# First four MLP units on half the tokens during the last normalisation, then on the other half

## The reference

```python
o = o @ w_out[l]
x = x + gt_a * rms_norm(o, g_post_attn[l])

h = rms_norm(x, g_pre_mlp[l]) * (1.0 + sc_m) + sh_m
y = jnp.square(jax.nn.relu(h @ w_mlp_in[l])) @ w_mlp_out[l]
x = x + gt_m * rms_norm(y, g_post_mlp[l])
```

## Time and profile before

| | before |
|---|---|
| median of 3 runs | 2115.51 us (2113.52 to 2116.0) |
| the profiled execution: its own time | 2116.55 us |
| its span, first to last instruction | 2114.9 us |
| PE busy | 2061.8 us, 97% |
| DVE busy | 1497.9 us, 71% |
| ACT busy | 844.0 us, 40% |
| mean granted TensorE clock | 0.991 |

### The profile page before, as it was taken

The page is one execution under the profiler, slowest core; times in us unless marked ns, Lnnn a source line. Parts: engine busy times, 40 slices in busy tenths (PEclk is TensorE's granted clock), DMA queues, the critical chain, the costliest instruction groups (busy, mean ns, idle before and its releaser), DMA issues.

```text
span 2114.9 us, 26212 instructions
## 1 busy us (share of the span) xinstructions
PE 2061.8 (97%) x9314; PEld 1703.6 (81%) x9314; DVE 1497.9 (71%) x1804; ACT 844.0 (40%) x1153; POOL 151.3 (7%) x159
## 2 busy tenths in 40 slices
PE   6999999999999989999999999999999999999998
PEld 6787888887788878888888888888788888888886
DVE  5986898788877776445544554435789888888866
ACT  4454322587732363333222332233333333333422
POOL 0000000038600000000000000012000000000000
PEclk8999999999999999999999999999999999999999
DMA  8997868600277737655665566676657356456442
GB/s 296 341 307 221 274 202 251 197 22 11 91 258 251 245 123 249 206 189 200 223 222 186 182 218 228 201 237 224 246 225 265 135 214 258 151 206 238 179 179 80
DMA packets 214353, 435.20 MB, mean 206 GB/s; under 512 B 30180, under 2 KB 69768, under 8 KB 205448
## 3 DMA queue, kind: packets, MB, share of 16 engines
q1 hardware_dynamic: 196136, 361.43, 50.8%
q0 software_dynamic: 16704, 67.11, 8.9%
q10 hardware_dynamic: 1440, 5.70, 0.7%
HBM read 367.09 MB, written 67.11 MB: 205 GB/s over the span
## 4 chain that ended last, share of the span: by engine, by line
PE 83%; DVE 7%; DMA 3%; issue 3%; ACT 3%; POOL 1%; SPq 0%; DVEq 0%; ACTq 0%; POOLq 0%
PE bank L2085 11%; PE bank L2087 11%; PE bank L2086 11%; PE bank L2522 7%; PE bank L2523 7%; PE bank L2524 7%; PE bank L2072 6%; PE bank L2074 6%; PE bank L2073 6%; DMA raw<-in_w_ada 1%; PE bank L2573 1%; PE bank L2571 1%; PE bank L2572 1%; DMA w<-in_w_mlp_out 1%; PE bank L2143 1%
## 5 line engine op out<-in xcount | busy, mean ns | idle before, releaser
L1241 DVE TENSOR_TENSOR lo<-raw,hi 128x1024 fp32r<-128x1024 f32 (+2 forms) x234 | 275.6, 1182 | 377.2 <-ACT hi L728 375.2
L728 ACT ACTIVATE hi<-raw 128x1024 fp32r<-128x1024 f32 (+2 forms) x236 | 239.4, 1023 | 657.5 <-PE bank L2087 410.7
L2085 PE MATMUL bank<-h_hi,hi 128*128 128x512 f32 x1016 | 396.0, 390 | 0.0
L2087 PE MATMUL bank<-h_hi,lo 128*128 128x512 f32 x1016 | 395.3, 389 | 0.0
L2086 PE MATMUL bank<-h_lo,hi 128*128 128x512 f32 x1016 | 395.2, 389 | 0.0
L2522 PE MATMUL bank<-hi,y_use 128*128 128x512 f32 x784 | 307.6, 392 | 7.7 <-DVE acc L1968 3.8
L2523 PE MATMUL bank<-lo,y_use 128*128 128x512 f32 x784 | 306.2, 391 | 0.0
L2524 PE MATMUL bank<-hi,y_use 128*128 128x512 f32 x784 | 306.1, 390 | 0.0
L1184 ACT ACTIVATE hi<-w 128x1024 fp32r<-128x1024 f32 x168 | 178.3, 1062 | 296.8 <-PE bank L2524 218.3
L1892 DVE TENSOR_TENSOR lo<-w,hi 128x1024 fp32r<-128x1024 f32 x168 | 204.0, 1219 | 37.6 <-ACT hi L1184 37.1
L2085 PEld LDWEIGHTS bank<-h_hi,hi 128*128 128x128 f32 x1016 | 190.7, 188 | 40.1 <-issue 0.6
(11 more groups left out here) (319 smaller groups left out, 3114.2 us busy)
## 6 DMA issues: line engine op xcount, KB each, us to landing
raw<-in_w_ada SPq DMA_DIRECT2D x192, 512.0 KB, 5.0
raw<-in_w_mlp_in SPq DMA_DIRECT2D x128, 512.0 KB, 4.4
w<-in_w_mlp_out SPq DMA_DIRECT2D x128, 512.0 KB, 5.2
y_dram<-y_out POOLq DMA_DIRECT2D x32, 1792.0 KB, 8.8
y_use<-y_dram SPq DMA_DIRECT2D x53, 1024.0 KB, 8.9
raw<-in_w_in SPq DMA_DIRECT2D x32, 512.0 KB, 5.6
raw<-in_w_out SPq DMA_DIRECT2D x32, 512.0 KB, 5.0
raw<-in_w_in SPq DMA_DIRECT2D x48, 256.0 KB, 5.4
```

The lines of the kernel that those rows point to most:

```text
L728: ins = nc.scalar.activation(dst, src, ACT.Copy)
L1241: ins = tt(dst, src, high.bitcast(F32), ALU.subtract)
L2085: mm(acc[n][:], wh, act_hi[:, k, :], start=first and q == 0, stop=False)
L2087: ins = mm(acc[n][:], wl, act_hi[:, k, :], start=False, stop=last and q == QROWS - 1)
```

## The change

Units 0 to 3 of the MLP's up-projection (k = 0 to 7) are done in two halves of 256 tokens: first on tiles 0 and 1, then on tiles 2 and 3, with 256 moving columns per product. The list TURNED holds the 24 transposed pieces in order: i = 0 to 7 are k = 0 to 7 for the first half, i = 8 to 15 the same k for the second half, i = 16 to 23 are k = 8 to 15 for all 512 tokens. PE makes the first three transposes inside the products of tile 3, behind unit 6 of the output projection. ACT (h2_high) and DVE (h2_middle, h2_low) make the pieces in an order in which the first half's pieces stand between the steps of tiles 2 and 3: in ACT's list h2_high(0) and (1) around the second square of tile 2, h2_high(2) and (3) ahead of tile 3's squares; in DVE's list h2_two(0) ahead of tile 3's sum, h2_two(2) ahead of its residual. For even i ACT makes the high part and the middle value (gain and shift applied); for odd i DVE makes the middle value and ACT copies it. The splits of units 0 to 3 move to other places in both lists; scaling of tile 1's 1536 columns goes behind tile 2's squares. The squares of the last block go to a free buffer in SBUF (ga_acc), each waiting for the one before. The diff, cut to its core:

```diff
@@ -120,8 +120,10 @@
 MLP_RAW_FIRST = MLP_RAW - MLP_RAW_N + MLP_N + 2 * GATE_N
 MLP_RAW_LAST = MLP_RAW_FIRST + MLP_RAW_N * (GROUPS - 1)
 MLP_RAW_END = MLP_RAW_LAST + MLP_N
-FIRST_AFTER = {3: [1], 7: [2, 3], 11: [4, 5]}
 FIRST_SPLIT = 6
+FIRST_K = KD // 2
+TURNED = [(k, half) for half in range(2) for k in range(FIRST_K)] + [(k, None) for k in range(FIRST_K, KD)]
+TURNED_N = len(TURNED)
...
         half_rows = (slice(0, ROPE_B), slice(ROPE_B, P))
         qr_hi_at = lambda pair, m: qr_stack[half_rows[m], pair % 2, m, :]
         qr_lo_at = lambda pair, m: qr_stack[half_rows[1 - m], pair % 2, m, :]
+        def turned_at(i):
+            k, half = TURNED[i]
+            if half is None:
+                return k, slice(0, T), bank[4 + i % 4][:], h2_f32[i % 4][:]
+            cols = slice(half * HALF_T, (half + 1) * HALF_T)
+            return k, cols, bank[4 + i % 4][:, 0:HALF_T], h2_half[i % 4][:]
         block = ctx.enter_context(nc.Block())
         O_ORDER = [*range(KD // 2, KD), *range(KD // 2)]
...
@@ -1081,13 +1092,37 @@
                 act.wait_ge(b_sum, (NB - 1) * 4 + t + 1)
                 if t == 0:
                     act.wait_ge(mod_read, MODS + 4)
-                if t >= 2:
-                    act.wait_ge(row_done, (NB - 1) * 4 + t - 1)
-                nc.scalar.activation(bank[2 + t % 2][:], part[:, t, :], ACT.Square, accum_out=row_sq[:, t, NB - 1:NB]).then_inc(row_done, 1)
+                if t:
+                    act.wait_ge(row_done, (NB - 1) * 4 + t)
+                nc.scalar.activation(ga_acc[:, 0, :], part[:, t, :], ACT.Square, accum_out=row_sq[:, t, NB - 1:NB]).then_inc(row_done, 1)
...
+            def x1_square(t, half):
+                act.wait_ge(x1_ready, 2 * t + half + 1)
+                cols = slice(half * HALF, (half + 1) * HALF)
+                nc.scalar.activation(z_tok[:, t, cols], x_res[:, t, cols], ACT.Square, accum_out=stat[:, t, 1 + half:2 + half]).then_inc(x1_sq, 1)
+                if half:
+                    act.dma_start(x1_d[t], x_res[:, t, :]).then_inc(x1_saved, 16)
+            def h2_high(i):
+                k, cols, src, mid = turned_at(i)
+                dst, g, b = h2_hi[:, k, cols], gsc_m[:, k:k + 1], shf_m[:, k:k + 1]
+                if i % 2 == 0:
+                    act.wait_ge(xn_turned, i + 1)
+                    if i >= 2 * FIRST_K:
+                        act.wait_ge(h2_ready, max(2 * FIRST_K, i - 3))
+                    elif i >= 4:
+                        act.wait_ge(h2_ready, i - 3)
+                    nc.scalar.activation(dst, src, ACT.Identity, scale=g, bias=b).then_inc(h2_hi_done, 1)
+                    nc.scalar.activation(mid, src, ACT.Identity, scale=g, bias=b).then_inc(h2_mid, 1)
+                else:
+                    act.wait_ge(h2_mid, i + 1)
+                    nc.scalar.activation(dst, mid, ACT.Copy).then_inc(h2_hi_done, 1)
             for t in range(NT):
                 square_last(t)
@@ -1097,30 +1132,32 @@
                 if t:
                     act.wait_ge(x1_rstd, t)
                     scale_x1(t - 1, slice(0, COLS), xn_ready)
-                    if t < NT - 1:
-                        scale_x1(t - 1, slice(COLS, D), xn_rest)
-                    else:
-                        split_hi(*at_mlp(0, 0))
-                for half in range(2):
-                    act.wait_ge(x1_ready, 2 * t + half + 1)
-                    cols = slice(half * HALF, (half + 1) * HALF)
-                    nc.scalar.activation(z_tok[:, t, cols], x_res[:, t, cols], ACT.Square, accum_out=stat[:, t, 1 + half:2 + half]).then_inc(x1_sq, 1)
-                act.dma_start(x1_d[t], x_res[:, t, :]).then_inc(x1_saved, 16)
+                if t == 1:
+                    scale_x1(0, slice(COLS, D), xn_rest)
+                if t == 2:
+                    split_hi(*at_mlp(0, 0))
+                if t == 3:
+                    h2_high(2)
+                    h2_high(3)
+                x1_square(t, 0)
+                if t == 2:
+                    h2_high(0)
+                x1_square(t, 1)
+                if t == 2:
+                    h2_high(1)
+                    split_hi(*at_mlp(0, 1))
+                    scale_x1(1, slice(COLS, D), xn_rest)
+            split_hi(*at_mlp(0, 2))
             root(2 * NT, NT - 1, 1)
-            scale_x1(NT - 2, slice(COLS, D), xn_rest)
-            for k in range(KD):
...
+            for i in range(4, 2 * FIRST_K):
+                h2_high(i)
+                if i == 5:
+                    split_hi(*at_mlp(0, 3))
+                    scale_x1(2, slice(COLS, D), xn_rest)
+            for i in range(2 * FIRST_K, TURNED_N):
+                h2_high(i)
+                if i in (2 * FIRST_K + 1, 2 * FIRST_K + 5):
+                    split_hi(*at_mlp(0, 4 + (i - 2 * FIRST_K) // 4))
...
@@ -1792,38 +1829,60 @@
                     cols = slice(half * HALF, (half + 1) * HALF)
                     stt(x_res[:, t, cols], z_tok[:, t, cols], rstd[:, t, 0:1], x_res[:, t, cols], ALU.mult, ALU.add).then_inc(x1_ready, 1)
+            def h2_middle(i):
+                k, _, src, mid = turned_at(i)
+                dve.wait_ge(xn_turned, i + 1)
+                if i >= 4:
+                    dve.wait_ge(h2_hi_done, i - 3)
+                dve.wait_ge(h2_mid, i)
+                ts(mid, src, gsc_m[:, k:k + 1], shf_m[:, k:k + 1], ALU.mult, ALU.add).then_inc(h2_mid, 1)
+            def h2_low(i):
+                k, cols, _, mid = turned_at(i)
+                dve.wait_ge(h2_mid, i + 1)
+                dve.wait_ge(h2_hi_done, i + 1)
+                tt(h2_lo[:, k, cols], mid, h2_hi[:, k, cols].bitcast(F32), ALU.subtract).then_inc(h2_ready, 1)
+            def h2_two(i):
+                h2_middle(i + 1)
+                h2_low(i)
+                h2_low(i + 1)
             for t in range(NT):
                 if t < NT - 1:
                     dve.wait_ge(b_tile, t + 1)
                 else:
+                    split_lo(*at_mlp(0, 0))
+                    h2_two(0)
                     dve.wait_ge(w_used, MLP_W)
                 sum_tile(NB - 1, t)
                 gate_tile(NB - 1, t)
                 if t:
                     x1_variance(t - 1)
+                if t == NT - 1:
+                    split_lo(*at_mlp(0, 1))
                 z_variance(t)
                 if t:
                     x1_factor(t - 1)
+                if t == NT - 1:
+                    h2_two(2)
                 residual(t)
-            split_lo(*at_mlp(0, 0))
+            split_lo(*at_mlp(0, 2))
             x1_variance(NT - 1)
+            h2_two(4)
             x1_factor(NT - 1)
...
-                    split_lo(*at_mlp(0, j))
+            ts(z_tok[:, NT - 1, 0:COLS], x_res[:, NT - 1, 0:COLS], rstd[:, NT - 1, 1:2], None, ALU.mult).then_inc(xn_ready, 1)
+            split_lo(*at_mlp(0, 3))
+            h2_two(6)
+            ts(z_tok[:, NT - 1, COLS:D], x_res[:, NT - 1, COLS:D], rstd[:, NT - 1, 1:2], None, ALU.mult).then_inc(xn_rest, 1)
+            for i in range(FIRST_K, TURNED_N, 2):
+                h2_two(i)
+                if i in (2 * FIRST_K, 2 * FIRST_K + 4):
+                    split_lo(*at_mlp(0, 4 + (i - 2 * FIRST_K) // 4))
...
+            def turn_x1(i):
+                k, half = TURNED[i]
+                _, _, dst, _ = turned_at(i)
+                tiles = range(NT) if half is None else (2 * half, 2 * half + 1)
+                for m, t in enumerate(tiles):
+                    ins = nc.tensor.transpose(dst[:, m * P:(m + 1) * P], z_tok[:, t, k * P:(k + 1) * P], ident[:])
+                ins.then_inc(xn_turned, 1)
             out_block(0, first=True)
             with pe.Fori(1, NB - 1) as n:
                 out_block(n)
@@ -2451,6 +2519,11 @@
                         ins.then_inc(w_used, 1)
                     elif j == 7:
                         ins.then_inc(b_tile, 1)
+                    if t == NT - 1 and j == 6:
+                        pe.wait_ge(xn_ready, 2)
+                        pe.wait_ge(b_sum, 4 * (NB - 1) + 3)
+                        for i in range(3):
+                            turn_x1(i)
                 if t == 0:
                     spread_ga(NB - 1)
                     pe.wait_ge(mod_summed, MODS + 4)
...
-            def first_columns():
-                w = at_mlp(0, 0)[1]
+            def first_columns(half, j):
+                r, w = at_mlp(0, j)
                 s = w.slot()
-                pe.wait_ge(raw_used, at_mlp(0, 0)[0].count(1, 1))
-                pe.wait_ge(h2_hi_done, 1)
...
-                    mm(bank[n][:], wh, h2_lo[:, 1, :], start=False, stop=False)
-                    ins = mm(bank[n][:], wl, h2_hi[:, 1, :], start=False, stop=False)
-                ins.then_inc(w_used, 1)
+                cols = slice(half * HALF_T, (half + 1) * HALF_T)
+                pe.wait_ge(raw_used, r.count(1, 1))
+                for q in range(QROWS):
+                    k = QROWS * j + q
+                    i = FIRST_K * half + k
+                    pe.wait_ge(h2_hi_done, i + 1)
```

(89 more changed lines are left out.)

17 lines of the change are left out of this document (removed).

## The result

Over 20 runs of each kernel the changed one takes 2118.66 us (median; 2114.72 to 2121.27) and the kernel before 2114.34 us (2111.22 to 2119.39). The ratio is 1.0017, interval 1.0011 to 1.0023: some 3.6 us slower (0.0017 x 2114.3), inside the 0.2% that I counted as no change. The profiled execution took 2116.49 us, with a span of 2114.8.

A forecast was written before the change was run, and what follows sets the result against it. PE was taken to bound the kernel, busy 2061.8 of 2114.9 us. The stretch to unit 8 grows from 60.41 to 64.0 us, +1.3 products and +2.3 loss, giving 2119.1 us median, range 2114.0 to 2124.5.

The forecast's parts named there:

- residual(3): DVE's residual of tile 3, behind h2_two(2): claimed to begin at 763.6 us where it begins at 757.27 before the change.
- k = 4: First-half products after k = 3: PE idle 5.3 us, start at 770.7 us at half clock, 1.8 us lost with k = 5.
- unit 8: First unit of the up-projection's second half, end of the compared stretch: claimed to start near 818.5 us, before 814.99.
- PE idle, all waits: PE waiting for ACT and DVE between tile 3's products and unit 8: 0.4, 0.6, 2.1, 0.4, 5.3 and 1.5 us.
- half clock and small pieces: Same stretch: 1.8 us at k = 4 and 5, plus 0.6 for some seven changes between transposes and products.
- part 1: Units 0 to 3: 192 products of 256 columns at 0.120 us replace 96 of 512 at 0.2267, +1.28 us.
- The one-column row: Trace row of 16 one-column products with weight loads, 0.107 us each: taken to show that 190 ns load records don't set pace.
- part 2: Walk through ACT, DVE and PE lists feeding the first half: 12.0 us idle and half clock, plus 0.6 for changes.
- part 3: Squares to SBUF, unchanged transposes and moved weight loads: claimed to cost nothing; a failed cover would show 5 us ahead of unit 8.
- Rival 1: Units 0 to 3: half products paced by their weight load, 0.188 us each, products +14.3 us, about 2127; chance 0.15.
- Rival 3: Units 0 to 3: the split does not matter, half products at 0.107 us and short operations quicker, 2117.5 us; chance 0.12.
- Rival 2: Tile 3's chain: h2_two(2) doesn't hold back residual(3), 9.6 us of loss gone, 2109.5 us, half of it 2114.3; chance 0.13.

The follow-up runs named there:

- e1b: The kernel before, with units 1 to 15 of the first MLP group in products of 256 columns, operands ready as before: ratio 1.0017 to before.
- e2: The changed kernel with one step of DVE's list moved, residual(3) ahead of h2_two(2): ratio 1.0015 to the kernel before.
- e8: The kernel before with only the last block's squares sent to SBUF, each waiting for the one before it: ratio 0.9997 to before.
- e5: The changed kernel reordered as in e4, with the splits of units 4 to 9 and gate loads also in the lists: 2109.01 us, 0.9975 to before.
- e4: The changed kernel with the same steps and half products in another written order on ACT, DVE and PE: ratio 0.9993 to the kernel before.

## Why the prediction was right

Forecast 2119.1 us, in the likeliest case 1.3 us of products and 2.3 of loss; 2118.7 came. The steps, with 3.65 us added to the times of after:

| step | forecast | measured |
|---|---|---|
| pace of half products | 0.120 us | 0.120 (after, e1b) |
| k = 0 | 755.5 | 755.7 |
| k = 2 | 761.6 to 761.7 | 761.6 |
| residual(3) | 763.6 | 763.6 |
| k = 4 | 770.7 | 770.6 |
| k = 6 | 775.4 | 775.8 |
| unit 8 | 818.5 | 819.2 |
| PE idle, all waits | 10.3 | 6.6 |
| half clock and small pieces | 2.4 | 6.6 |
| loss (small changes included) | 12.6 | 13.2 |

**The products** (part 1) cost what the sum said: half of a product's 0.213 and the same 0.013 on top. The one-column row was the one to trust, not the recorded length of a weight load.

**The chain** (part 2) came within 0.1 us up to k = 4. Identity of 256 columns took 0.55 us, the middle 0.54, the low 0.42, the copy 0.42 for 0.40. That h2_two(2) holds back residual(3) is in the trace of after, and e2 shows in its trace what that alone costs: 3.0 of the 5.7 us by which residual(3) is later than before, and 1.6 us of the stretch, which the time of e2 neither confirms nor denies.

**Idle time against half clock.** Here the terms were off and their sum wasn't: 10.3 us of idle time and 2.4 of half clock and small pieces stood in the sum, and 6.6 and 6.6 came. I had 5.3 us idle before k = 4 and 1.8 of loss behind it. It was 3.76 idle, because k = 2 and 3 already ran in part at half clock (0.67 over 757.9 to 763.0) and so ended later, and more was lost at half clock behind it (0.50 from 768 to 770). Operands that come at a fixed time make the two interchangeable: what PE loses by being slow it would else have waited. I had said that the low clock comes at 771 to 774; on the time scale of before it was seen from 762.4 to 765.6 (758.7 to 762.0 in after) and from 770.9 to 775.8. Behind k = 4 that doesn't hold, and there it is in part luck that the errors cancel: k = 4 and 5 lost 2.4 us for my 1.8, and from k = 6 on PE waited 0.7 us for my 1.5, but lost about 1.1 us more than I had reckoned in small pieces. The trace ran another 0.3 us behind there; that is the 0.7 at unit 8.

The stretch is 4.2 us longer in the profiles where the ratio says 3.6 (2.3 to 4.9); the difference is within the scatter of a stretch.

**What costs nothing** (part 3): the squares' new place (e8), and the weight loads. No wait for a DMA stands in PE's waits of after.

**The rivals.** Rival 1 fell with the pace. Rival 3 asked for 0.107 and fell too. Rival 2 was wrong of this order, and right of the idea: it said that 96 half products could cover tile 3, and that the strict order on DVE and ACT speaks against it. e5 has the same steps in another order and gains 9 us on the changed kernel. That this is near the 9.6 that rival 2 reckoned is chance: its condition, an early residual(3), doesn't hold in e5 (8.03). What I did not see is that the order, and not the split, was what could be repaired.

## What to carry to other kernels

Splitting products so that the tensor engine can start on the tokens that are ready costs the fixed part of each product once more (0.013 us here, 1.3 us in all) and moves work of two in-order engines ahead of the chain on which the rest waits. Whether that pays is decided by the written order: the same steps lost 3.6 us in one order and gained 5.3 in another. Write the lists of all engines side by side, walk them with durations from the trace, put every later step that shares the engines into the walk too (e4 lost 2.1 us of waiting and 1.6 of half clock to one that was left out), and only then judge the split.
